# Linear attention in a fused layer: another order of the steps, state increments per head, updates over all partitions

## The reference, cut to what matters

```python
q, k, v, log_a = rs(q) * (dk ** -0.5), rs(k), rs(v), rs(log_a)     # chunks of 64 tokens
b = jnp.cumsum(log_a, axis=3)
b_last = b[:, :, :, -1:, :]
q_dec, k_inv, k_end = q * jnp.exp(b), k * jnp.exp(-b), k * jnp.exp(b_last - b)
attn = jnp.einsum('bhcld,bhcmd->bhclm', q_dec, k_inv) * mask
o_intra = jnp.einsum('bhclm,bhcmv->bhclv', attn, v)
chunk_kv = jnp.einsum('bhcld,bhclv->bhcdv', k_end, v)
decay = jnp.exp(b_last[:, :, :, 0, :])
def step(s, inp):
    qd, kv, dc = inp
    o = jnp.einsum('bhld,bhdv->bhlv', qd, s)
    return dc[..., None] * s + kv, o
```

## Time and profile before

| | us |
|---|---|
| median of 3 runs | 1922.54 |
| lowest, highest | 1921.53, 1926.82 |
| the profiled execution: its time | 1922.93 |
| its span | 1921.1 |
| mean granted TensorE clock | 0.95 |
| TensorE busy | 1733.5 (90%) |
| VectorE busy | 937.5 (49%) |
| ScalarE busy | 838.4 (44%) |

### The profile page before, as it was taken

How to read it: one execution, slowest core, us unless ns; L and a number is a source line. 1 busy time by engine, 2 the same in 40 slices (tenths; PEclk the granted TensorE clock), 3 DMA queues, 4 the chain that set the end, 5 groups by cost and what they waited for, 6 DMA issues and landing times.

```text
span 1921.1 us, 30384 instructions
## 1 busy us (share of the span) xinstructions
PE 1733.5 (90%) x8430; PEld 1356.8 (71%) x8431; DVE 937.5 (49%) x1462; ACT 838.4 (44%) x949; POOL 774.6 (40%) x452
## 2 busy tenths in 40 slices
PE   5899999978899988799998998999999979999845
PEld 1767788867645576678887877888888868888622
DVE  6522310167656884344454455533654654466419
ACT  0521011421012342366565566645665665567512
POOL 3520000400000447167446556635666556546620
PEclk9899999988699999899999999999999989999868
DMA  9505531020434353489789989967998899989776
GB/s 340 176 23 167 171 112 36 14 88 1 174 143 152 102 211 99 158 269 321 227 282 287 316 264 334 277 181 201 326 319 260 262 296 325 254 253 308 245 218 270
DMA packets 104719, 406.48 MB, mean 212 GB/s; under 512 B 17837, under 2 KB 36394, under 8 KB 76513
## 3 DMA queue, kind: packets, MB, share of 16 engines
q1 hardware_dynamic: 63360, 284.10, 40.1%
q0 software_dynamic: 37424, 107.59, 23.2%
q10 hardware_dynamic: 3888, 14.16, 2.2%
HBM read 339.94 MB, written 84.72 MB: 221 GB/s over the span
## 4 chain that ended last, share of the span: by engine, by line
PE 57%; DMA 20%; DVE 8%; issue 5%; POOL 4%; ACT 4%; SPq 1%; ACTq 1%; DVEq 0%; POOLq 0%
PE ps L832 27%; PE ps L1891 11%; DMA raw<-w_exp_up 8%; DMA arena<-hx_dram,arena 6%; PE ps L2022 5%; PE ps L887 3%; POOL list_dram L565 3%; DMA acc_dram<-arena 2%; DMA arena<-w_ada 2%; PE ps L1839 2%; DVE arena L1713 1%; POOL d_split L571 1%; PE ps L1976 1%; PE ps L1864 1%; PE ps L2015 1%
## 5 line engine op out<-in xcount | busy, mean ns | idle before, releaser
L832 PE MATMUL ps<-gu_split,xT 128*128 (+1 forms) x2712 | 637.1, 391 | 0.0
L832 PEld LDWEIGHTS ps<-gu_split,xT 128*128 128x128 f32 x2712 | 510.6, 189 | 106.8 <-issue 0.4
L832 PE MATMUL ps<-d_split,hTe 128*128 (+1 forms) x1356 | 354.9, 412 | 34.0 <-ACT arena L708 33.7
L571 POOL TENSOR_TENSOR d_split<-raw,d_split (+1 forms) x65 | 299.4, 4606 | 199.5 <-ACT d_split L632 198.4
L961 DVE TENSOR_TENSOR gu_split<-raw,gu_split (+1 forms) x130 | 294.4, 2306 | 132.2 <-ACT gu_split L627 132.2
L832 PEld LDWEIGHTS ps<-d_split,hTe 128*128 128x128 f32 x1356 | 257.6, 196 | 89.7 <-issue 38.4
L627 ACT ACTIVATE gu_split<-raw (+1 forms) x130 | 241.2, 1906 | 71.0 <-SPq L479 65.2
L589 POOL DMA_INDIRECT arena<-hx_dram,arena x108 | 138.8, 1285 | 192.9 <-DVE arena L1132 144.5
L1126 DVE TENSOR_TENSOR arena<-ps,arena 128x256 f32<-128x256 f32 x113 | 70.5, 624 | 294.9 <-ACT arena L714 294.7
L598 POOL DMA_INDIRECT acc_dram<-arena x104 | 171.9, 1653 | 89.3 <-DVE arena L1137 56.5
L1891 PE MATMUL ps<-hT_split,w_split 128*128 128x512 f32 (+1 forms) x816 | 192.7, 394 | 3.7 <-DVE w_split L1572 3.7
(11 more groups left out here) (284 smaller groups left out, 1507.6 us busy)
## 6 DMA issues: line engine op xcount, KB each, us to landing
raw<-w_exp_gate SPq DMA_DIRECT2D x64, 1024.0 KB, 8.4
raw<-w_exp_up SPq DMA_DIRECT2D x64, 1024.0 KB, 12.0
raw<-w_exp_down SPq DMA_DIRECT2D x64, 1024.0 KB, 7.5
arena<-w_ada SPq DMA_DIRECT2D x16, 1024.0 KB, 4.9
arena<-acc_dram SPq DMA_DIRECT2D x18, 512.0 KB, 18.2
arena<-w_ada SPq DMA_DIRECT2D x4, 2048.0 KB, 27.9
w_raw<-w_in SPq DMA_DIRECT2D x16, 512.0 KB, 4.8
acc_dram<-arena POOLq DMA_DIRECT2D x1, 5120.0 KB, 16.6
```

The source lines that it names most:

```text
L571: tt(d_split(q, 1), raw_d(q), d_split(q, 0).bitcast(F32), ALU.subtract).then_inc(d_low, 1)
L832: last = mm(dst, lhs(a, j), rhs(b, j), start=(t == 0), stop=(t == len(terms) - 1))
```

## The change

Five edits, all in the linear attention stage.

1. In VectorE's loop the scaling of tile s comes first in step s, ahead of the masks of s-1. The scaling of ke is one operation over 512 columns instead of two over 256, and only it waits for the transposed k.
2. e1 has three buffers instead of two, at the start of the first region; ScalarE's wait for the states is one tile looser.
3. TensorE's decays and transposes of k are put into functions. Tile 0's come ahead of the loop; those of s+1 come in step s, the decays after the increments, the transposes after the output.
4. The increments are computed per head: 32 matmul instructions of 64x64 blocks in the trace for a tile instead of 16 of 64x128, and the blocks off the diagonal are never written. VectorE clears banks 3 and 4 once, before ft_done. The updates then run over 128 partitions and 128 columns, 8 for a tile instead of 16.
5. The two mask operations are one over 1024 columns.

```diff
--- before.py
+++ after.py
@@ -172,7 +172,7 @@
         bs, bm = carve(R1, FT_TEMP, 2, 4, P), carve(R1, FT_TEMP + CW, 2, 4, P)
         bpq, buv = carve(R1, FT_TEMP + 2 * CW, 2, 2, P), carve(R1, FT_TEMP + 2 * CW + 512, 2, 2, P)
         G0 = EW
-        e1 = carve(R0, G0, 2, 4, P)
+        e1 = carve(R0, 0, 3, 4, P)
         ki = carve(R0, G0 + 1024, 2, 4, P)
         ke = carve(R0, G0 + 2048, 2, 512)
         qd = carve(R0, G0 + 3072, 3, 4, P)
@@ -1501,10 +1501,11 @@
 
             for u in range(NT):
                 act.wait_ge(bg_mm, u + 1)
+                if u >= 3:
+                    act.wait_ge(S_ready, 2 * (u - 2))
                 if u >= 2:
-                    act.wait_ge(S_ready, 2 * (u - 1))
                     act.wait_ge(kv_mm, u - 1)
-                a(e1[:, u % 2].rearrange("p a b -> p (a b)"), ps[:, 1, :], ACT.Exp).then_inc(e_ready, 1)
+                a(e1[:, u % 3].rearrange("p a b -> p (a b)"), ps[:, 1, :], ACT.Exp).then_inc(e_ready, 1)
                 a(ki[:, u % 2].rearrange("p a b -> p (a b)"), ps[:, 1, :], ACT.Exp, scale=-1.0).then_inc(e_ready, 1)
                 a(ke[:, u % 2], ps[:, 2, :], ACT.Exp).then_inc(e_ready, 1)
 
@@ -1678,20 +1679,35 @@
             dve.wait_ge(ft_mm, 9)
             for j in range(2):
                 for h in range(2):
-                    dve.tensor_copy(yT[:, 6 + j, 0:SAMPLE].rearrange("p (c d) -> p d c", d=8)[:, 4 * h:4 * h + 4, :],
-                                    ps[:, 2 + 2 * j + h, :].rearrange("p (d c) -> p d c", d=4))
+                    last = dve.tensor_copy(yT[:, 6 + j, 0:SAMPLE].rearrange("p (c d) -> p d c", d=8)[:, 4 * h:4 * h + 4, :],
+                                           ps[:, 2 + 2 * j + h, :].rearrange("p (d c) -> p d c", d=4))
+            done(last)
+            dve.memset(ps[:, 3:5, :], 0.0)
             dve.tensor_copy(yT[:, 6:8, SAMPLE:T], ps[:, 6, 0:2 * P].rearrange("p (j c) -> p j c", j=2))\
                .then_inc(ft_done, 1)
 
             for s in range(NT + 2):
+                u = s
+                if u < NT:
+
+                    dve.wait_ge(e_ready, 3 * (u + 1))
+                    if u >= 3:
+                        dve.wait_ge(o_mm, u - 2)
+                    for d in range(2):
+                        cols = tile(ft_tile(u, d))
+                        pr = slice(2 * d, 2 * d + 2)
+                        dve.tensor_tensor(qd[:, u % 3, pr], qT[:, :, cols], e1[:, u % 3, pr], ALU.mult)
+                        dve.tensor_tensor(ki[:, u % 2, pr], kT[:, :, cols], ki[:, u % 2, pr], ALU.mult)
+                    dve.wait_ge(k_t, u + 1)
+                    dve.tensor_tensor(ke[:, u % 2, :], ps[:, 0, :], ke[:, u % 2, :], ALU.mult).then_inc(qk_ready, 1)
                 u = s - 1
                 if 0 <= u < NT:
 
                     dve.wait_ge(attn_mm, u + 1)
                     if u >= 2:
                         dve.wait_ge(o_mm, u - 1)
-                    dve.tensor_tensor(am[:, u % 2, 0], ps[:, 5, :], C["mask"], ALU.mult)
-                    dve.tensor_tensor(am[:, u % 2, 1], ps[:, 6, :], C["mask"], ALU.mult).then_inc(am_ready, 1)
+                    dve.tensor_tensor(am[:, u % 2], ps[:, 5:7, :], C["mask"].unsqueeze(1).to_broadcast((P, 2, 512)), ALU.mult)\
+                       .then_inc(am_ready, 1)
 
                     dve.wait_ge(kv_mm, u + 1)
                     if u == 0:
@@ -1707,12 +1723,10 @@
                             c = half if d == 0 else 1 - half
                             edge = 64 * c + (63 if d == 0 else 0)
                             for q in range(2):
-                                for h in range(2):
-                                    hs = slice(h * 64, (h + 1) * 64)
-                                    x = 2 * d + q
-                                    last = dve.scalar_tensor_tensor(
-                                        new[hs, x, hs], old[hs, x, hs], e1[hs, u % 2, x, edge:edge + 1],
-                                        ps[hs, 3 + c, x * P + h * 64:x * P + (h + 1) * 64], ALU.mult, ALU.add)
+                                x = 2 * d + q
+                                last = dve.scalar_tensor_tensor(
+                                    new[:, x, :], old[:, x, :], e1[:, u % 3, x, edge:edge + 1],
+                                    ps[:, 3 + c, x * P:(x + 1) * P], ALU.mult, ALU.add)
                         last.then_inc(S_ready, 1)
                 u = s - 2
                 if 0 <= u < NT:
@@ -1731,21 +1745,6 @@
                                 dve.wait_ge(o_acc, u)
                             last = dve.tensor_tensor(dst, src, dst, ALU.add)
                     last.then_inc(o_acc, 1)
-                u = s
-                if u < NT:
-
-                    dve.wait_ge(e_ready, 3 * (u + 1))
-                    dve.wait_ge(k_t, u + 1)
-                    if u >= 3:
-                        dve.wait_ge(o_mm, u - 2)
-                    for d in range(2):
-                        cols = tile(ft_tile(u, d))
-                        pr = slice(2 * d, 2 * d + 2)
-                        dve.tensor_tensor(qd[:, u % 3, pr], qT[:, :, cols], e1[:, u % 2, pr], ALU.mult)
-                        dve.tensor_tensor(ki[:, u % 2, pr], kT[:, :, cols], ki[:, u % 2, pr], ALU.mult)
-                        last = dve.tensor_tensor(ke[:, u % 2, d * W:(d + 1) * W], ps[:, 0, d * W:(d + 1) * W],
-                                                 ke[:, u % 2, d * W:(d + 1) * W], ALU.mult)
-                    last.then_inc(qk_ready, 1)
 
             dve.wait_ge(o_acc, NT)
             o = o_tm.rearrange("p i w -> p (i w)")
@@ -1952,19 +1951,30 @@
             pe.wait_ge(la_ready, 4)
             pe.wait_ge(setup_in, GATE_IN)
             pe.wait_ge(v_ready, NT)
+            def decays(u):
+
+                if u:
+                    pe.wait_ge(e_ready, 3 * u)
+                for x in range(4):
+                    mm(ps[:, 1, x * P:(x + 1) * P], la[u][:, x * P:(x + 1) * P],
+                       C["cum"][:, (x // 2) * P:(x // 2 + 1) * P], start=True, stop=True)
+                for d in range(2):
+                    last = mm(ps[:, 2, d * W:(d + 1) * W], C["suf"][:, d * P:(d + 1) * P], la[u][:, d * W:(d + 1) * W],
+                              start=True, stop=True)
+                last.then_inc(bg_mm, 1)
+
+            def turn_k(u):
+
+                if u:
+                    pe.wait_ge(qk_ready, u)
+                for d in range(2):
+                    for j in range(2):
+                        last = pe.transpose(ps[:, 0, d * W + j * P:d * W + (j + 1) * P], kT[:, j, tile(ft_tile(u, d))], ident)
+                last.then_inc(k_t, 1)
+
+            decays(0)
+            turn_k(0)
             for s in range(NT + 2):
-                u = s
-                if u < NT:
-
-                    if u:
-                        pe.wait_ge(e_ready, 3 * u)
-                    for x in range(4):
-                        mm(ps[:, 1, x * P:(x + 1) * P], la[u][:, x * P:(x + 1) * P],
-                           C["cum"][:, (x // 2) * P:(x // 2 + 1) * P], start=True, stop=True)
-                    for d in range(2):
-                        last = mm(ps[:, 2, d * W:(d + 1) * W], C["suf"][:, d * P:(d + 1) * P], la[u][:, d * W:(d + 1) * W],
-                                  start=True, stop=True)
-                    last.then_inc(bg_mm, 1)
                 u = s - 1
                 if 0 <= u < NT:
                     pe.wait_ge(qk_ready, u + 1)
@@ -1978,21 +1988,17 @@
                     last.then_inc(attn_mm, 1)
                     if u:
                         pe.wait_ge(S_ready, 2 * u)
-                    for c in range(2):
-                        for x in range(4):
+                    for x in range(4):
+                        for c in range(2):
                             rows = slice(c * 64, (c + 1) * 64)
-                            last = mm(ps[:, 3 + c, x * P:(x + 1) * P], ke[rows, u % 2, x * P:(x + 1) * P],
-                                      v_tm[rows, ft_tile(u, x // 2), (x % 2) * P:(x % 2 + 1) * P], start=True, stop=True)
+                            for h in range(2):
+                                at = x * P + h * 64
+                                vcols = slice((x % 2) * P + h * 64, (x % 2) * P + (h + 1) * 64)
+                                last = mm(ps[h * 64:(h + 1) * 64, 3 + c, at:at + 64], ke[rows, u % 2, at:at + 64],
+                                          v_tm[rows, ft_tile(u, x // 2), vcols], start=True, stop=True, skip_group_check=True)
                     last.then_inc(kv_mm, 1)
-                u = s
-                if u < NT:
-
-                    if u:
-                        pe.wait_ge(qk_ready, u)
-                    for d in range(2):
-                        for j in range(2):
-                            last = pe.transpose(ps[:, 0, d * W + j * P:d * W + (j + 1) * P], kT[:, j, tile(ft_tile(u, d))], ident)
-                    last.then_inc(k_t, 1)
+                if s + 1 < NT:
+                    decays(s + 1)
```

(3 more changed lines are left out.)

## The result

The changed kernel takes 1875.71 us (median of 4 runs, 1874.42 to 1877.09) against 1922.03 us for the one before: ratio 0.9769, 95% interval 0.9748 to 0.979, 46.3 us less. The forecast was 1887 with a range of 1879 to 1907. In a second comparison, on another chip, the ratio was 0.9763 (0.9729 to 0.9796) and the median 1874.85 us.

The account below looks back on a forecast made before the run. Scaling, scores and masks in series between VectorE and TensorE bound the linear attention stage. With TensorE steps of 8.5 us it would end at 480.0 instead of 516.3; net gain 36, so 1922.9 - 36 gives 1887 us, range 1879 to 1907.

Parts of the forecast that it names:

- The series of scaling, scores and masks: In each old linear attention step these three lie in series, with TensorE standing still 2.85 us before the scores.
- TensorE's step: TensorE's work per tile in the linear attention: 8.0 + 0.2 + 0.34 = 8.5 us, bounds 7.9 and 9.7, setting the step.
- the increments: TensorE's 32 new increment instructions per tile: 0.05 us each, 1.6 us in all, bounds 1.0 and 2.75.
- handshakes: Waits between engines in the linear attention stage: 1.6 us taken back from the gain, leaving 36 us net.
- The gaps at a change of tiling: On TensorE around the increments, where array tile columns change: 2 x 0.17 us added per step.
- VectorE's step: VectorE's scaling, masks, states and output per tile: 6.9 us, bounds 6.7 and 7.5, below TensorE's 8.5.
- The clock: TensorE's clock in the linear attention: without idle stretches it should stay at 2.4 GHz once up.
- The rival that it never rises: Clock stays low throughout the stage: TensorE takes 15.7 us a step, time 1949 us; chance 0.08.
- Clearing: VectorE's one-time memset of two banks before ft_done, with its wait: 1.1 us on the path, bounds 0.6 and 2.
- Warm projection: The output projection after the stage begins at the higher clock; starting at the lower one had cost about 1.3 us.
- Late next: After the stage nothing else becomes late, so the gain of 36 us should reach the end whole.
- The range: Forecast time 1879 to 1907 us, chance about 0.82; its low end took increments at 1.0 us without drains.

Follow-up runs that it names:

- e1: Not a run but a buffer in the kernel's code, read by the state updates; the change gives it three buffers instead of two.
- one_quadrant: Changed kernel with the same 32 increment instructions per tile, sorted so eight in a row use the same array quadrant: step 8.5 us, ratio to before 0.983.
- order_only: Kernel before with only the new places of scaling, decays and transposes and the third e1 buffer: stage 93.3 us, ratio to before 0.9872.
- small_updates: Changed kernel with the 16 state updates of 64x64 per tile put back: stage 89.1 us, step 8.6 us, ratio to before 0.9844.
- before_filled_more: Kernel before with constant matmuls in TensorE's waits for the scaling, 20 in each, 46 in the first: stage 106.0 us, ratio to before 0.9939.

## Why the prediction was wrong, by its own steps

**The series of scaling, scores and masks: right.** It was the bound, and it was broken up; VectorE waits for TensorE, 1.60 us a step where I had written 1.4 to 1.5.

**TensorE's step: right in kind, 8.5 for 7.61.** The term that failed is the increments: 1.6 us, with a lower bound of 1.0, and it was 0.62. I took the rate from line 2008, where two column halves alternate, and halved it for the halved moving columns. The row had the overlap of two tiles in it, but I did not ask what four would do. one_quadrant gives 1.47 us for these instructions without overlap, close to my 1.6, so the price of an instruction was sound and the overlap was missed. The rest of the step's sum, start to start: the scores took 1.64 where 2.75 less 1.4 left 1.35 for them, since part of the old increments had run beside them, and the last decays' tail was 0.2 us shorter than I had it. These two nearly cancel, so the 0.9 us by which a step is below its sum are the increments. From the first decays to the projection my sum has 80.7 us (399.3 to 480.0), and it was 72.5: 8.2 of the 11.2 us between forecast and time. 1.6 more are the handshakes below; the last 1.6 or so lie outside of the stage and are less than the spread of the runs (1874.42 to 1877.09, before 1915.00 to 1926.82). The Trainium skill, "TensorEngine Tiling (Array Packing)", Key Properties, says that different tiles can load weights and multiply in parallel. I had quoted it and put the sum only some 4 us lower by it, since I tied it to the same bound. Here the runs agree with the page, with 0.020 us an instruction on four tiles in turn against 0.046 on one.

**The gaps at a change of tiling: half right.** I added 0.34 us beside the increments. There is none ahead of line 1997 and none behind it, although the tile changes at both places. Instead 0.17 stands ahead of the scores, which in the kernel before lay inside the idle time, and the gap ahead of the state output grew from 0.17 to 0.33. The sum is 0.33 more than before, the same as I had, at other places.

**VectorE's step: 5.98 for 6.9.** Masks 1.22, output 0.76 and the wide product 0.69 came as priced from their rows, though from start to start each is up to 0.1 shorter than its recorded length. The updates took 2.27 for 8, 0.28 from start to start, where I had 0.36. The recorded length (344 ns on average) was as the row said; the distance between two was not length plus a gap. It cost the forecast nothing, since VectorE has slack.

**The clock: right.** It rose between 405 and 406 and was 1.00 to the end of the stage. The runs with filled waits show that idle TensorE had been the cause of the falls within the steps. The rival that it never rises is out.

**Clearing: 1.3 us for 1.1.** The memset itself was 0.91, its wait 0.29, and the copy behind it starts 1.3 us later than before. **Warm projection: right,** about 1.3 us. **The 1.6 us that I took back for handshakes** did not show: in the steady steps there is no idle TensorE at all. It is a second, smaller part of the miss.

**Late next: right.** The projection starts 41.2 us earlier (516.3 to 475.1), the first matmul on the lists 42.6 (777.2 to 734.6), the experts' last summation 48.5 (1863.4 to 1814.9): nothing of the gain was given back, and the 7 us on top are not traced to the change.

**The range** ended at 1879 because its low end was built from the wrong lower bound of a single term. (By its own words it would be 1880.7: 0.9 x 7 is 6.3 less than 1887.) With 0.62 for the increments in nine tiles, 8.8 less, and without the 1.6 for handshakes the same sum gives 1876 to 1877.

## What to carry to other kernels

When two engines hand work to and fro within a step, put what the other engine waits for first, work a step ahead, and compare the sums of the two engines: the longer one is the new step. Matmuls that use only a quadrant of the array should be issued so that neighbours lie on different quadrants; the order alone made a factor of 2.3 here. Idle stretches cost twice where they lower the clock: here, filling gaps of 2 to 5 us on TensorE with useless work won 12 us of the stage, so such a kernel has more to win than the gaps themselves. The end of a stage counts too: where TensorE waited for the last states, order_only and small_updates lost 8 to 10 us there.

## What the runs showed of the hardware that was not expected

- 64x64 float32 matmul instructions with 64 moving columns: 0.046 us each on one quadrant, 0.028 with two in turn (rows or columns alike), 0.020 with four (1.47, 0.90 and 0.62 us for 32).
- A VectorE update of 128 partitions by 128 columns follows its predecessor after 0.28 us, one of 64 by 64 after 0.294 (4.71 for 16, small_updates). A quarter of the elements was not cheaper at all; the cause was not looked for.
- The kernel before became faster by 0.6% (0.4 to 0.8) from matmuls that compute nothing.
- One and the same program took 1920 us on some chips and 1950 on others. 20 of the 30 us lie between the first projection matmul and the first on the experts' lists (260.9 us in the kernel before on a chip of the first kind, 280.6 in before_filled_more on one of the second).
